# MLP up products of a two-layer trunk with the weight tile stationary and the activations moving

## The reference

```python
def sqrelu_mlp(h, w_up, w_down):
    return jnp.square(jax.nn.relu(h @ w_up)) @ w_down

for layer in range(DEPTH):
    h = h + (fox_mixer if layer % 2 == 0 else retention_mixer)(rmsnorm(h, norm[layer]), ...)
    h = h + sqrelu_mlp(rmsnorm(h, mlp_norm[layer]), mlp_up[layer], mlp_down[layer])
return rmsnorm(h, final_norm)
```

## Time and profile before

| what | value |
|---|---|
| median of the runs | 2603.72 us |
| span of the profiled execution | 2602.8 us, which is 0.9 us less than the median; the page has no time of its own for this execution beside the span |
| TensorE matmul busy | 2583.9 us (99%) |
| TensorE weight load busy | 2136.2 us (82%), lies beside the matmuls |
| VectorE / ScalarE busy | 1396.4 us (54%) / 1194.6 us (46%) |
| DMA, mean busy share | about 0.55, 186 GB/s |
| granted TensorE clock | 0.999 of full speed over the span |

### The profile page before, as it was taken

One profiled execution on the slowest core, in us unless ns is written; L12 is line 12 of the kernel. 1 busy time (PEld: TensorE's weight loads), 2 busy tenths in 40 slices (PEclk: granted clock), 3 DMA queues, 4 the chain that ended last, 5 costly groups with the idle time before them and its releaser, 6 DMA issues.

```text
span 2602.8 us, 34966 instructions
## 1 busy us (share of the span) xinstructions
PE 2583.9 (99%) x11770; PEld 2136.2 (82%) x11770; DVE 1396.4 (54%) x1565; ACT 1194.6 (46%) x1446; POOL 36.7 (1%) x43
## 2 busy tenths in 40 slices
PE   8999999999999999999999999999999999999998
PEld 6888888888888888888888888888888888888887
DVE  5545455555555555565555555555555455555554
ACT  6445444444434434455455344445444344443443
POOL 0000000000000000000000000000000000000000
PEclk9999999999999999999999999999999999999999
DMA  6545456555555555565555655555555555555554
GB/s 231 175 140 170 153 194 203 181 192 181 188 194 180 186 193 190 194 210 176 180 188 194 199 189 175 175 194 183 177 197 188 192 185 187 192 193 193 194 186 137
DMA packets 132851, 483.41 MB, mean 186 GB/s; under 512 B 15025, under 2 KB 15297, under 8 KB 132033
## 3 DMA queue, kind: packets, MB, share of 16 engines
q1 hardware_dynamic: 131040, 474.81, 54.6%
q0 software_dynamic: 1760, 7.87, 0.9%
HBM read 480.53 MB, written 2.10 MB: 185 GB/s over the span
## 4 chain that ended last, share of the span: by engine, by line
PE 99%; ACT 0%; DMA 0%; DVE 0%; SPq 0%; issue 0%; ACTq 0%; DVEq 0%
PE acc L353 31%; PE acc L355 31%; PE acc L354 31%; PE tr L371 2%; DMA raw<-in_w_stream 0%; PE sc L455 0%; PE sc L592 0%; PE sc L454 0%; PE sc L453 0%; PE mix L607 0%; PE mix L605 0%; PE mix L606 0%; PE mix L463 0%; ACT w_hi L654 0%; PE sc L416 0%; PE tr L479 0%
## 5 line engine op out<-in xcount | busy, mean ns | idle before, releaser
L924 DVE TENSOR_TENSOR w_lo<-raw,w_hi 128x1024 fp32r<-128x1024 f32 x896 | 1076.0, 1223 | 443.1 <-ACT w_hi L654 414.5
L654 ACT ACTIVATE w_hi<-raw 128x1024 fp32r<-128x1024 f32 x896 | 931.6, 1058 | 603.8 <-PE acc L355 340.0
L353 PE MATMUL acc<-w_hi,xT_hi 128*128 128x512 f32 x2176 | 864.0, 397 | 3.9 <-DVE w_lo L924 3.2
L355 PE MATMUL acc<-w_hi,xT_lo 128*128 128x512 f32 x2176 | 848.9, 390 | 0.0
L354 PE MATMUL acc<-w_lo,xT_hi 128*128 128x512 f32 x2176 | 847.4, 389 | 0.0
L353 PE MATMUL acc<-w_hi,aT_hi 128*128 128x512 f32 x1408 | 550.9, 391 | 0.1
L355 PE MATMUL acc<-w_hi,aT_lo 128*128 128x512 f32 x1408 | 548.1, 389 | 0.0
L354 PE MATMUL acc<-w_lo,aT_hi 128*128 128x512 f32 x1408 | 547.7, 389 | 0.0
L355 PEld LDWEIGHTS acc<-w_hi,xT_lo 128*128 128x128 f32 x2176 | 408.8, 188 | 87.1
L353 PEld LDWEIGHTS acc<-w_hi,xT_hi 128*128 128x128 f32 x2176 | 409.1, 188 | 86.0 <-issue 3.8
L354 PEld LDWEIGHTS acc<-w_lo,xT_hi 128*128 128x128 f32 x2176 | 409.5, 188 | 80.8
(11 more groups left out here) (134 smaller groups left out, 600.9 us busy)
## 6 DMA issues: line engine op xcount, KB each, us to landing
raw<-in_w_stream SPq DMA_DIRECT2D x896, 512.0 KB, 4.4
gain<-in_gains POOLq DMA_DIRECT2D x4, 1024.0 KB, 6.7
scratch<-in_gn POOLq DMA_DIRECT2D x8, 256.0 KB, 5.4
scratch<-in_decay POOLq DMA_DIRECT2D x8, 192.0 KB, 3.3
h<-in_x SPq DMA_DIRECT2D x4, 256.0 KB, 5.2
h<-in_x SPq DMA_DIRECT2D x1, 1024.0 KB, 11.0
out<-raw SPq DMA_DIRECT2D x1, 1024.0 KB, 3.9
out<-raw SPq DMA_DIRECT2D x4, 256.0 KB, 2.5
```

Source lines behind the costliest of these rows:

```text
L353: pe.matmul(acc[tok][:, :], hi_t[:, x_cols], w_hi[:, w_cols], start=(kt == 0), stop=False)
L355: m = pe.matmul(acc[tok][:, :], lo_t[:, x_cols], w_hi[:, w_cols], start=False, stop=(kt == KT - 1))
L654: act.activation(w_hi[:, s * SW:(s + 1) * SW], raw[:, s % RAW * SW:(s % RAW + 1) * SW], ACT.Copy).then_inc(hi_made, 1)
L924: dve.tensor_tensor(w_lo[:, c], raw[:, s % RAW * SW:(s % RAW + 1) * SW], w_hi[:, c].bitcast(F32), ALU.subtract).then_inc(lo_made, 1)
```

## The change

The up products change sides. The 128 x 128 weight tile becomes the stationary operand and the activations move, high and low part side by side: `w_hi` against `[x_hi | x_lo]` of all 256 tokens (512 columns) and `w_lo` against `x_hi` (256 columns). The result has 128 hidden channels on the partitions and tokens in the columns, which is the form that the down products want as `aT`; columns 0 to 255 of the bank hold the main sum and columns 256 to 511 w_hi x_lo. ScalarE copies the latter out (`low_out`), VectorE adds, then does max(x, 0) x in one instruction, ScalarE makes the high part, VectorE the low part (`up_made`). The up products of a block use two slots for each of four groups (`UPS`) of 128 hidden channels; each group fills one bank and each slot is given back once. The weights of up blocks are laid out anew in HBM (same bytes, same slots). The transposes of up results go; those into `xT` stay, and the pending one stands after the first slot of the MLP's first up block. `xT` and `aT` hold high and low part of each 128-channel piece side by side. Down products and mixers keep their matmuls.

```diff
-        xT_hi, xT_lo = sb("xT_hi", TOKS * D, F32R), sb("xT_lo", TOKS * D, F32R)
-        aT_hi, aT_lo = sb("aT_hi", TOKS * D, F32R), sb("aT_lo", TOKS * D, F32R)
+        xT, aT = sb("xT", 2 * TOKS * D, F32R), sb("aT", 2 * TOKS * D, F32R)
...
+        def piece(buf, kt, part, tok=None):
+            start = (2 * kt + part) * S
+            return buf[:, start:start + S] if tok is None else buf[:, start + tok * P:start + (tok + 1) * P]
...
@@ TensorE, product()
+                    if fresh == "by ups" and tok == 0:
+                        pe.wait_ge(up_made, T("up") - KT + (s + 1) * PER_SLOT)
...
+            def up_block(first=None):
+                for j in range(UPS):
+                    bank = acc[j % 2]
+                    for s in (2 * j, 2 * j + 1):
+                        if s == 2 * j:
+                            wait(pe, acc_out[j % 2], T("acc", j // 2))
+                        pe.wait_ge(lo_made, T("block") * SLOTS + (s + 1))
+                        if first and s == 1:
+                            first()
+                        for kk in range(KT // 2):
+                            kt = s % 2 * (KT // 2) + kk
+                            if first and s == 1 and kt == KT - NB // P:
+                                for t in range(TOKS):
+                                    pe.wait_ge(tr_out[t], T(f"tr{t}"))
+                            w_cols = slice(s * SW + kk * P, s * SW + (kk + 1) * P)
+                            both = xT[:, 2 * kt * S:2 * (kt + 1) * S]
+                            pe.matmul(bank[:, :], w_hi[:, w_cols], both, start=(kt == 0), stop=False)
+                            m = pe.matmul(bank[:, 0:S], w_lo[:, w_cols], piece(xT, kt, 0), start=False,
+                                          stop=(kt == KT - 1))
+                        if s % 2:
+                            m.then_inc(acc_done[j % 2], 1)
+                        else:
+                            m.then_inc(w_used, 1)
...
             def mlp(last):
-                run_block(xT, pending, own, fresh=True)
+                up_block(first=pending)
...
-                    ups(i)
-                    run_block(aT, pending, fresh=True)
-                    T.loop(pe, QUADS - 1, lambda i: run_block(aT), block=1)
-                    run_block(xT, None, own)
+                    run_block(aT, fresh="by ups")
+                    T.loop(pe, QUADS - 1, lambda i: run_block(aT), block=1, acc=1)
+                    ups(QUADS)
...
@@ ScalarE
             def up_block(u):
-                acc_to(0, evac[0][:, :], ACT.Relu, 1.0)
-                split(0, 2)
-                batch_hi(0, aT_hi, u)
-                split(2, 7)
-                acc_to(1, evac[1][:, :], ACT.Relu, 1.0)
-                split(7, 8)
-                T.up("block")
-                batch_hi(1, aT_hi, u)
+                for j in range(UPS):
+                    b = j % 2
+                    split(2 * j, 2 * j + 1, ups=True)
+                    act.wait_ge(acc_done[b], T("acc", j // 2 + 1))
+                    act.activation(evac[b][:, 0:S], acc[b][:, S:2 * S], ACT.Copy).then_inc(low_out, 1)
+                    split(2 * j + 1, 2 * j + 2, ups=True)
+                    act.wait_ge(up_squared, T("up", j + 1))
+                    act.activation(aT[:, bass.ds((u * UPS + j) * 2 * S, S)], stage[b][:, S:2 * S],
+                                   ACT.Copy).then_inc(up_hi, 1)
...
@@ VectorE
             def up_block(u):
-                def squares(tok):
-                    dve.wait_ge(acc_out[tok], T("block", 1))
-                    dve.tensor_tensor(stage[tok][:, :], evac[tok][:, :], evac[tok][:, :],
-                                      ALU.mult).then_inc(staged[tok], 1)
-                squares(0)
-                split(0, 2)
-                batch_lo(0, aT_hi, aT_lo, u)
-                split(2, 7)
-                squares(1)
-                split(7, 8)
-                T.up("block")
-                batch_lo(1, aT_hi, aT_lo, u)
+                for j in range(UPS):
+                    b = j % 2
+                    total, sq = stage[b][:, 0:S], stage[b][:, S:2 * S]
+                    split(2 * j, 2 * j + 1)
+                    dve.wait_ge(low_out, T("up", j + 1))
+                    dve.tensor_tensor(total, acc[b][:, 0:S], evac[b][:, 0:S], ALU.add).then_inc(acc_out[b], 1)
+                    dve.wait_ge(acc_out[b], T("acc", j // 2 + 1))
+                    dve.scalar_tensor_tensor(sq, total, 0.0, total, ALU.max, ALU.mult).then_inc(up_squared, 1)
+                    split(2 * j + 1, 2 * j + 2)
+                    dve.wait_ge(up_hi, T("up", j + 1))
+                    at = (u * UPS + j) * 2 * S
+                    dve.tensor_tensor(aT[:, bass.ds(at + S, S)], sq, aT[:, bass.ds(at, S)].bitcast(F32),
+                                      ALU.subtract).then_inc(up_made, 1)
```

More of the change, by code:

```diff
@@ L413, in forget_gate @@
                     f_cols = slice(kt * 2 * FOX_HEADS, kt * 2 * FOX_HEADS + P)
-                    for x_t in (xT_hi, xT_lo):
-                        x_both = x_t[:, :].rearrange("p (t d) -> p t d", t=TOKS)[:, :, kt * P:(kt + 1) * P]
-                        m = pe.matmul(z, wf_split[:, f_cols], x_both, start=(kt == 0 and x_t is xT_hi),
-                                      stop=(kt == KT - 1 and x_t is xT_lo))
+                    for part in range(2):
+                        m = pe.matmul(z, wf_split[:, f_cols], piece(xT, kt, part), start=(kt == 0 and part == 0),
+                                      stop=(kt == KT - 1 and part == 1))
                 m.then_inc(gate_done, 1)
@@ L550, in _ @@
             run_block(xT, mix_pending, k_own)
-            T.loop(pe, GROUPS - 2, group_and_k, block=3, tr0=3, tr1=3, group=1)
+            T.loop(pe, GROUPS - 2, group_and_k, block=3, acc=3, tr0=3, tr1=3, group=1)
             run_block(xT, k_pending, q_own_and_cum)
@@ L639, in _, with next_block, split @@
         def _(act):
-            T = Tally("block", "tr0", "tr1", "squared", "group", "ret_head", "norm")
-            def split(first, last, block0=False):
+            T = Tally("block", "acc", "used", "up", "tr0", "tr1", "squared", "group", "ret_head", "norm")
+            def next_block():
+                T.up("block")
+                T.up("acc")
+                T.up("used", SLOTS - 1)
+            def split(first, last, block0=False, ups=False):
                 for s in range(first, last):
@@ L797, in add_block @@
                 if normed:
-                    act.wait_ge(acc_out[0], T("block", 1))
+                    act.wait_ge(acc_out[0], T("acc", 1))
                     square(0, n)
@@ L909, in _, with next_block @@
         def _(dve):
-            T = Tally("block", "hi0", "hi1", "step", "norm", "mixer_norm", "group", "ret_head")
+            T = Tally("block", "acc", "up", "hi0", "hi1", "step", "norm", "mixer_norm", "group", "ret_head")
+            def next_block():
+                T.up("block")
+                T.up("acc")
             def step(ins):
@@ L1242, in _ @@
             for t in range(TOKS):
-                dve.wait_ge(acc_out[t], T("block"))
+                dve.wait_ge(acc_out[t], T("acc"))
                 for n in range(QUADS - 1):
```

218 lines of the change are left out of this document (121 added, 97 removed).

## The result

Twenty runs of each kernel: 2603.48 us before, 2607.89 us after (2605.49 to 2611.46). The ratio is 1.0017 with a 95% interval of 1.0010 to 1.0024: the change makes the kernel slower by 4.4 us (0.17%; the interval leaves out 1), where 12.2 us less were forecast. The profiled execution has a span of 2605.9 us against 2602.8.

A forecast was written before the change was run, and what follows sets the result against it. TensorE was taken to bound the kernel: 2602.8 - 29.8 (transposes) + 10.9 (pairs) + 6.7 (waits) = 2590.6 us of span, 2591.5 us as median, 12.2 us less. Forecast band 2588 to 2595, range 2580 to 2601.

The forecast's parts named there:

- What bounds: Whole kernel: TensorE sets the time, with matmuls on 99% of the span; other engines count only where it waits.
- what goes: 32 up blocks lose two batches of four transposes each, 64 of 136 batches: 29.8 us less on TensorE.
- The pair: Up blocks: a 512- plus a 256-column matmul costs 226.7 + 118.7 = 345.4 ns, adding 10.9 us over 32 blocks.
- the margin against it: Short matmul in up blocks: at 124.6 ns instead of 118.7 the kernel is no longer faster; the margin is 6 ns.
- Rival (a): Up blocks: the next weight load does not hide behind a short matmul, pair 0.415 us, time 2734 us; chance 0.08.
- My own sign for it: Up blocks in the profile after: pairs repeating at more than 351 ns would make the forecast fall and Rival (a) hold.
- The waits: First up block of each MLP: TensorE waits for the pending tile and then `tr_out`, 3.35 us each, 6.7 us together.
- Banks, ScalarE, VectorE, DMA: Up blocks and steps between block kinds: engine work, slot supply and bank release fit in time, costed at nothing.
- Rival (d): Step from down to up blocks: addition 2.5 us later, about 1 us wait at 6 places, 2597.5 us; chance 0.08.
- (b): Up blocks: the pair costs no more than its columns, 113.3 ns for the short one, 2580.6 us; chance 0.12.
- (c): MLPs' starts: the waits do not come, since slot 6 or the addition comes earlier, 2584.8 us; chance 0.08.

The follow-up runs named there:

- first kernel: TensorE alone, without the trunk: sixteen patterns of fp32r matmuls, each with its own weight load; 256 columns alone took 120.0 ns, 512 and 256 in turns 353.4 ns per pair.
- early batch kernel: Changed kernel with the second half's addition, square, gain and transposed tile ahead of slots 6 and 7's splits before each MLP: 2599.73 us, ratio to before 0.9985.
- experiment 10: Early batch kernel with one up block's first 16 matmuls reordered in each chunk behind down blocks, not in MLPs' first chunks: 2590.16 us, ratio to before 0.9944.
- experiment 9: Changed kernel with the first 16 matmuls of one up block per chunk reordered (LLSSLLSSLSLSLSLS), waits left in: 2597.55 us, ratio to before 0.9974.

## Why the prediction was wrong, step by step

- **What bounds, what goes: right.** TensorE, 64 batches. Their 29.8 us are not seen alone in any run, but both sums below close with them.
- **The pair: wrong, and this is the step that failed** ("the change of size adds nothing", "an up block 64 x 0.3454 = 22.10 us"). Measured are 1792 pairs of 353.3 and 256 of 346.7 ns, 721.9 us against 696.4 us for 3072 matmuls of 226.7: 25.5 us more instead of 10.9. Of the 14.6 us missed, 1792 x 6.6 = 11.8 us are the slow rhythm, and 2048 x 1.3 = 2.7 us come from taking the mean of the forget gate's 32 matmuls, 118.7, where the pace of a long run is 120.0 (first kernel, and 346.7 - 226.7). The gate's row could not show the rest: it has 256 columns only, and the price arises where both lengths take turns. I had written the margin against it down as 6 ns, named the load as the only cause that could use it up, and gave it 0.08. Measured are 7.9 ns more per pair than I forecast: 1.3 in the short matmul's own pace and 6.6 in the alternation.
- **Rival (a), the load: not confirmed, and not excluded as a part.** My own sign for it, pairs above 351 ns, came true, but it could not tell the load from a price of the alternation. The load at full length behind each short matmul would give 415 ns, and short matmuls alone, each with its load, take 120 ns. But with 64 weight columns on either side the pair takes 340 ns, and short ones alone 113.3 instead of 120.0, so the size of the weight tile has a part in these times.
- **The waits: right in place, one of the two prices too low.** Forecast were 3.35 us each. The first MLP's first chunk takes 93.71 us from first to last long matmul, where 90.09 + 0.47 for transposes was due: 3.15 us. The second takes 94.70 where 88.40 + 0.47 was due: 5.8 us, since the granted clock fell for some 7 us after 1.99 us of idle time. The prediction had no term for that. The early batch kernel takes all but some 0.25 us of each wait away, and its clock did not fall.
- **Banks, ScalarE, VectorE, DMA: right.** No idle time of TensorE in any later up block.
- **The sum with measured terms:** -29.8 + 25.5 + 9.0 = 4.7 us; the first MLP's start is 1.8 us earlier (423.68 instead of 425.44, a lead that TensorE has from its first 24 us on, while the first weights arrive), so 2.9, and the spans differ by 3.1. For the kernel of experiment 10: 1792 pairs of 346.7, 256 of 353.3, 15.3 us; with -29.8 this is -14.5 us, and the two starts still cost 0.7 us (89.59 and 91.21 us for the first chunks, where 89.21 and 90.91 were due), so -13.8. The profiled spans differ by 13.7 us, and the medians by 0.0056 of 2603.5, 14.6 us.
- **Rival (d), (b), (c):** not seen. The range ended at 2601, since I gave the alternation itself no price. The chance of a faster kernel, stated as 0.87, adds up to 0.88 from its parts.

What stays open is why there are two rhythms. The difference is 6.6 ns in the pair, the same for 256 and 384 columns beside 512, and twice that in L L S. In the kernel before, too, the first long matmuls behind a batch of transposes were slower (the mean over the 127 batches with at least 13 long matmuls behind them is 232 ns for the third to seventh distance, and 226.7 from the eighth on), so slower distances end by themselves among long matmuls; whether that is the same state as the slow rhythm, no run shows. Open too is what decides the rhythm behind a wait. Which part of TensorE keeps the rhythm, no run here tells.

## What to carry to other kernels

A matmul's price in a mix of lengths is not that of each length alone: measure the very alternation, over 50 rounds, from several entries, before a plan turns on a few nanoseconds. If two stretches of the same code differ by a constant amount per round, change what stands ahead of the loop: here eight matmuls in another order, once in each of six chunks, were worth 10 us. And a new wait of 2 us on TensorE may cost more than its length, so a tile that was pending at leisure has to be made earlier on the other engines when its place in TensorE's queue moves up.

## What the runs showed of the hardware that was not expected

- Matmuls of 512 and 256 columns in turns take 346.7 or 353.3 ns per pair, for the same code, addresses and clock, and stay so for 256 pairs and across semaphore waits that were already met. Behind an unbroken run of long matmuls what stands ahead decides (18 of 18 chunks each way); behind a wait either came, 8 fast and 4 slow. The order by twos gave 348.0 to 348.3 in every trace.
- A good entry is not good everywhere: L L S S L L S S leads from long matmuls into the fast rhythm (in all 19 places in the traces), and from fast pairs into the slow one in three of four places (the fourth is the first MLP of experiment 9, which stayed fast).
- The granted clock fell to 0.50 for 3.4 to 6.8 us in five of the eight traced waits of this kind: after 1.88, 1.93, 1.94, 1.99 and 2.00 us of idle time, and not after 1.71, 1.83 and 2.03 us. The first chunks' rhythm and this fall of the clock are both places where executions can differ (the changed kernel 2605.5 to 2611.5 us; the early batch kernel 2599.2 to 2603.5), but with one trace of each kernel their shares are not shown.
